# HGRN levels of both directions in one product, and features jobs over side-by-side high and low activations

## The reference

```python
u = h @ w_in                                   # 2048 -> 5 x 2048
q, f_f, f_b, v, g = split(u)
f = lb + (1 - lb) * sigmoid(f_raw);  k = 1 - f # one f and k for each direction
# per head of 128, forward and, on reversed tokens, backward:
#   S_t = diag(f_t) S_{t-1} + k_t v_t^T,  o_t = S_t^T q_t
o = rmsnorm(o_forward + o_backward) * silu(g)
...
up = dwconv3(h @ ffn_w_in);  gate, val = split(up)
x = x + rmsnorm((silu(gate) * val) @ ffn_w_out)
```

## Time and profile before

| | |
|---|---|
| median of 3 runs | 2662.48 us (2662.04 to 2663.64) |
| profiled execution | 2662.26 us, span 2660.5 us |
| PE busy | 2621.0 us (99%) |
| VectorE busy | 1634.4 us (61%) |
| ScalarE busy | 1167.0 us (44%) |
| granted clock of TensorE, mean | 0.996 |
| read from HBM | 461.38 MB, 174 GB/s |

### The profile page before, as it was taken

How to read it: one execution, slowest core, us unless ns; L and a number is a source line. 1 busy time by engine, 2 the same in 40 slices (tenths; PEclk the granted TensorE clock), 3 DMA queues, 4 the chain that set the end, 5 groups by cost and what they waited for, 6 DMA issues and landing times.

```text
span 2660.5 us, 40147 instructions
## 1 busy us (share of the span) xinstructions
PE 2621.0 (99%) x17158; PEld 2391.8 (90%) x17158; DVE 1634.4 (61%) x1811; ACT 1167.0 (44%) x1330; POOL 27.7 (1%) x25
## 2 busy tenths in 40 slices
PE   7999999999999999999999999999899999999997
PEld 6879888998988989989999999988799999999996
DVE  6545656555555555555767667675666666666666
ACT  6544344443443444454333333424445444444443
POOL 0000000000000000000000000000000000000000
PEclk9999999999999999999999999999999999999999
DMA  9534445555555555555444343535455555555553
GB/s 358 170 135 153 159 151 189 182 183 194 185 187 193 183 190 190 182 184 181 143 143 151 127 166 119 181 121 182 143 199 189 183 187 186 184 189 183 186 186 112
DMA packets 127441, 466.09 MB, mean 175 GB/s; under 512 B 14208, under 2 KB 14464, under 8 KB 126368
## 3 DMA queue, kind: packets, MB, share of 16 engines
q1 hardware_dynamic: 127264, 463.54, 50.2%
HBM read 461.38 MB, written 2.10 MB: 174 GB/s over the span
## 4 chain that ended last, share of the span: by engine, by line
PE 67%; issue 32%; ACT 1%; DVE 0%; DMA 0%; POOL 0%; POOLq 0%; DVEq 0%; SPq 0%; ACTq 0%
PE job L676 33%; PE job L679 26%; PE att L861 4%; PE att L808 1%; PE att L708 0%; PE att L696 0%; ACT w_high L928 0%; PE att L872 0%; PE att L886 0%; PE att L889 0%; PE att L849 0%; PE att L776 0%; DMA raw<-in_weights 0%; PE att L726 0%; PE att L749 0%
## 5 line engine op out<-in xcount | busy, mean ns | idle before, releaser
L1176 DVE TENSOR_TENSOR w_low<-raw,w_high 128x1024 fp32r<-128x1024 f32 x856 | 1046.2, 1224 | 914.2 <-ACT w_high L928 912.7
L928 ACT ACTIVATE w_high<-raw 128x1024 fp32r<-128x1024 f32 x856 | 904.6, 1058 | 1258.7 <-PE job L676 638.3
L679 PE MATMUL job<-actA_high,w_high 128*128 128x256 f32 x3328 | 945.5, 284 | 1.0 <-issue 1.0
L679 PE MATMUL job<-actA_high,w_low 128*128 128x256 f32 x3328 | 942.9, 283 | 0.0
L679 PE MATMUL job<-actA_low,w_high 128*128 128x256 f32 x3328 | 942.9, 283 | 0.0
L679 PEld LDWEIGHTS job<-actA_high,w_high 128*128 128x128 f32 x3328 | 639.8, 192 | 2.1 <-issue 1.4
L679 PEld LDWEIGHTS job<-actA_high,w_low 128*128 128x128 f32 x3328 | 639.8, 192 | 0.7
L679 PEld LDWEIGHTS job<-actA_low,w_high 128*128 128x128 f32 x3328 | 639.7, 192 | 0.0
L676 PE MATMUL job<-w_high,actB_high 128*128 128x512 f32 x1184 | 464.4, 392 | 10.7 <-DVE w_low L1176 10.1
L676 PE MATMUL job<-w_low,actB_high 128*128 128x512 f32 x1184 | 462.1, 390 | 0.0
L676 PE MATMUL job<-w_high,actB_low 128*128 128x512 f32 x1184 | 461.8, 390 | 0.0
(11 more groups left out here) (197 smaller groups left out, 1214.2 us busy)
## 6 DMA issues: line engine op xcount, KB each, us to landing
raw<-in_weights SPq DMA_DIRECT2D x856, 512.0 KB, 3.3
M<-in_mem_t SPq DMA_DIRECT2D x4, 512.0 KB, 7.5
slots<-in_mem SPq DMA_DIRECT2D x2, 1024.0 KB, 14.3
M<-in_x_t SPq DMA_DIRECT2D x4, 512.0 KB, 13.2
H<-in_x SPq DMA_DIRECT2D x1, 2048.0 KB, 15.0
out<-H SPq DMA_DIRECT2D x4, 512.0 KB, 2.9
slots<-in_w_small SPq DMA_DIRECT2D x1, 1024.0 KB, 14.4
slots<-in_post_mix_g SPq DMA_DIRECT2D x1, 1024.0 KB, 5.6
```

The lines of the kernel that those rows point to most:

```text
L679: mm = nc.tensor.matmul(J[job.buf][:, x // 2, (x % 2) * T:(x % 2 + 1) * T], wt[:, slot, cc, x * P:(x + 1) * P], a[:, c, :], start=begins a ...
L928: nc.scalar.activation(w_high[:, s % AHEAD, :, :], raw[:, s % RAW_SLOTS, :, :], ACT.Copy)\
L1176: nc.vector.tensor_tensor(w_low[:, s % AHEAD, :, :], raw[:, s % RAW_SLOTS, :, :], w_high[:, s % AHEAD, :, :].bitcast(F32), ALU.subtract).t ...
```

## The change

It has three parts.

1. **Features jobs.** The high and low activations lie side by side for each chunk (`act_both`). Per block of weights, one instruction streams 512 columns (high and low activations) over the high weights, and one streams 256 columns (high activations) over the low weights into the second half of the same PSUM bank. A job has 256 output columns and 4 windows of four chunks; the number of windows stays. The two sums lie in the two halves of a bank and are added when the job is emptied (`join`: ScalarE copies one part to SBUF, VectorE adds the other); a `scale` over both halves follows where there was a product with `R4`.
2. **HGRN levels.** The levels of both directions are one product with 128 columns. The slots of the two directions are swapped so that one access pattern (`crossed`) takes in turn m columns of the one direction's queries and m of the other's; ScalarE copies the keys crossed in the same way into `sq` (`hgrn_keys`). A level stands behind every second window, base+27 to base+39; the stages after it move by two windows.
3. **FFN.** For the value jobs of blocks 1 to 9, `conv_side` moves by two windows, `y_mul` and `y_split` by four.

```diff
-WIN = 2
+        self.width = COLS if kind == "tokens" else T
+        self.per = 1024 // self.width
+        self.windows = len(self.rows) // self.per
...
+def feature_job(p, act, weight, col, needs, to, scaled):
+    for half in (0, 1):
+        j = p.job("features", act, weight, col + half * T, needs=needs)
+        p.put_early(j.end, "join", j.buf, to, half)
+    if scaled:
+        p.put_early(j.end, "scale", to)
+    return j
...
-        for i in range(2 * LEVELS):
-            p.put(base + 27 + i * 12 // 14, "hgrn_level", i // 2, i % 2)
+        for level in range(LEVELS):
+            p.put(base + 25 + 2 * level, "hgrn_keys", level)
+            p.put(base + 27 + 2 * level, "hgrn_level", level)
...
-        p.put(base + 39, "hgrn_across")
+        p.put(base + 41, "hgrn_across")
...
+        later = 2 if which == "value" and 0 < b < FFN_BLOCKS - 1 else 0
         p.put(j.end, "conv_mid", which, b)
-        p.put(j.end + 1, "conv_side", which, b)
+        p.put(j.end + 1 + later, "conv_side", which, b)
...
-            p.put(j.end + 1, "y_mul")
-            p.put(j.end + 2, "y_split", b)
+            p.put(j.end + 1 + 2 * later, "y_mul")
+            p.put(j.end + 2 + 2 * later, "y_split", b)
...
+        def crossed(slot, start, n, m):
+            base = slots[:, slot, start:start + n]
+            return bass.AP(base.tensor, base.offset, [list(base.ap[0]), [2 * m, n // (2 * m)], [1024 + m, 2], [1, m]])
+
+        def block_totals(slot, at, step, n, m):
+            base = slots[:, slot, at:at + 1]
+            return bass.AP(base.tensor, base.offset, [list(base.ap[0]), [2 * m, n // (2 * m)], [step, 2], [0, m]])
...
                         else:
+                            cols = slice(cc * T + x * P, cc * T + (x + 1) * P)
+                            nc.tensor.matmul(J[job.buf][:, x, :], w_high[:, slot, cols],
+                                             act_both[job.act][:, c, :, :].rearrange("p a t -> p (a t)"), start=begins, stop=False,
+                                             skip_group_check=True)
+                            mm = nc.tensor.matmul(J[job.buf][:, x, T:2 * T], w_low[:, slot, cols],
+                                                  act_high[job.act][:, c, :], start=False, stop=ends,
+                                                  skip_group_check=True)
...
-            def hgrn_level(level, direction):
+            def hgrn_level(level):
                 m = 1 << level
+                bank = 2 * (level % 2)
                 wait(pe, n, "diagonal", 0)
-                wait(pe, n, "stepped", -1)
+                wait(pe, n, "stepped", 0)
+                wait(pe, n, "keys_set", 0)
+                wait(pe, n, "picked", -1)
+                wait(pe, n, "o_low", 0)
...
+                        at = (2 * h + t) * P
+                        mm = nc.tensor.matmul(att[:, bank + at // COLS, at % COLS:at % COLS + P],
+                                              hg["sq"][:, at:at + P], crossed(0, h * T + t * P, P, m),
+                                              start=True, stop=True)
...
+                elif name == "join":
+                    buf, to, half_ = a
+                    x = by_feature(JOIN[to][:, half_ * COLS:(half_ + 1) * COLS])
+                    wait(dve, n, "low_copied")
+                    nc.vector.tensor_tensor(x, J[buf][:, :, 0:T], x, ALU.add).then_inc(S["joined"], 1)
+                elif name == "scale":
+                    x = by_feature(JOIN[a[0]])
...
+                    queries, keys = crossed(0, 0, 1024, m), crossed(2, 0, 1024, m)
+                    nc.vector.tensor_tensor(keys, keys, block_totals(7, 2 * m - 1, -1024 - m, 1024, m), ALU.mult)\
+                        .then_inc(S["keys_stepped"], 1)
+                    nc.vector.tensor_tensor(queries, queries, block_totals(6, 2 * m - 1, 1024 - m, 1024, m), ALU.mult)\
                         .then_inc(S["stepped"], 1)
+                    pick = sibling[:, level, :].unsqueeze(1).to_broadcast([P, 8, P])
+                    nc.vector.copy_predicated(heads8(hg["diag"]), pick, att[:, bank:bank + 2, :].rearrange(
+                        "p a (x c) -> p (a x) c", c=P)).then_inc(S["picked"], 1)
                     if level < LEVELS - 1:
-                        double(hg["f"][direction], m)
+                        dve.wait_ge(S["stepped"], n.at("stepped", 1))
+                        t = slots[:, 6:8, :].rearrange("p d (n two m) -> p d n two m", two=2, m=m)
+                        done(nc.vector.tensor_tensor(t[:, :, :, 1, m - 1], t[:, :, :, 0, m - 1], t[:, :, :, 1, m - 1],
+                                                     ALU.mult))
```

More of the change, by code:

```diff
@@ L196, in plan_inputs @@
                       ("gk", GK), ("gv0", GV), ("gv1", GV + COLS), ("gg0", GG), ("gg1", GG + COLS)):
-        j = p.job("features" if name in ("gq", "gk") else "tokens", "A", "w_in", col, needs=("low_made", X_SET))
+        if name in ("gq", "gk"):
+            j = feature_job(p, "A", "w_in", col, None, "gla_" + name[1], True)
+            if name == "gk":
+                p.put_early(j.end, "gla_make")
+            continue
+        j = p.job("tokens", "A", "w_in", col, needs=("low_made", X_SET))
         if name in ("fq", "fk", "mq"):
@@ L275, in plan_hgrn @@
         for direction in (0, 1):
-            j = p.job("features", "A", "hgrn_w_in", (1 + direction) * D + g * COLS, needs=needs)
+            j = feature_job(p, "A", "hgrn_w_in", (1 + direction) * D + g * COLS, needs, f"f{direction}", True)
             if g == 0 and direction == 0:
@@ L340, in up @@
         needs = ("low_made", PREFFN_SET) if b == 0 else None
[L341 to L342 removed]
+        j = feature_job(p, "A", "ffn_w_in", b * COLS + (FFN if which == "value" else 0), needs, "z", True)
+        later = 2 if which == "value" and 0 < b < FFN_BLOCKS - 1 else 0
         p.put(j.end, "conv_mid", which, b)
[L344 removed]
+        p.put(j.end + 1 + later, "conv_side", which, b)
         if which == "gate":
@@ L650, in window @@
                     once(*EMPTIED[job])
-                for cc in range(WIN):
-                    c = job.chunk(WIN * k + cc)
+                for cc in range(job.per):
+                    c = job.chunk(job.per * k + cc)
                     if job.needs:
@@ L659, in window @@
                         elif kind == "y_low":
-                            once(kind, job.rows[WIN * k + cc] // 4 + 1)
+                            once(kind, job.rows[job.per * k + cc] // 4 + 1)
                         elif which == "hgrn":
@@ new lines, in window @@
+                        c = job.rows[job.per * k + cc] % 8
+                    begins = k == 0 and cc == 0
+                    ends = k == job.windows - 1 and cc == job.per - 1
+                    for x in range(TT):
+                        if job.kind == "tokens":
+                            cols = slice(cc * COLS, (cc + 1) * COLS)
+                            ah, al = (a[job.act][:, c, x * P:(x + 1) * P] for a in (act_high, act_low))
+                            to = J[job.buf][:, x, :]
+                            nc.tensor.matmul(to, ah, w_high[:, slot, cols], start=begins, stop=False)
+                            nc.tensor.matmul(to, ah, w_low[:, slot, cols], start=False, stop=False)
+                            mm = nc.tensor.matmul(to, al, w_high[:, slot, cols], start=False, stop=ends)
+                        else:
+                            cols = slice(cc * T + x * P, cc * T + (x + 1) * P)
[5 more added lines that the diff above has]
+                                                  skip_group_check=True)
@@ L1635 @@
                "ffn_w_in": a["ffn_w_in_2"][0], "ffn_w_out": a["ffn_w_out_2"][0]}
-    weights = np.empty((PLAN.windows, P, WIN, COLS), np.float32)
-    for w, (j, k) in enumerate(WINDOW):
-        for cc in range(WIN):
-            r = j.rows[WIN * k + cc]
-            weights[w, :, cc, :] = sources[j.weight][r * P:(r + 1) * P, j.col:j.col + COLS]
+    weights = np.empty((PLAN.windows, P, 1024), np.float32)
+    for w, (job, k) in enumerate(WINDOW):
+        for cc in range(job.per):
+            r = job.rows[job.per * k + cc]
+            weights[w, :, cc * job.width:(cc + 1) * job.width] = (
+                sources[job.weight][r * P:(r + 1) * P, job.col:job.col + job.width])
     def turned(v):
```

205 lines of the change are left out of this document (84 added, 121 removed).

## The result

The changed kernel takes 2603.34 us (median of 4 runs, 2601.59 to 2604.82), the kernel before 2662.66 on the same chips: a ratio of 0.9774 (0.9763 to 0.9786). It is 59.3 us faster; I had said 90. The time lies 11 us above the range of 2565 to 2592. The profiled execution took 2601.59 us at a mean granted clock of 0.996, as before.

A forecast was written before the change was run, and what follows sets the result against it. TensorE's own work was taken as the bound: 2660.5 - 44.3 (features) - 50.8 (HGRN) + 2.0 + 2.5 + 0.8 = 2570.7 us of span, put at 2572.5 us for the time, with an 8-in-10 range of 2565 to 2592.

The forecast's parts named there:

- What bounds the kernel: Whole kernel: TensorE's own work bounds it, busy 2621.0 of 2660.5 us; faster work on other engines can bring little.
- rival D: Joins of the 104 features jobs: buffers not emptied in time, so slower than before, 2718 at 12.5 us an emptying; chance 0.03.
- Features jobs: Features windows: a pair of records costs 0.3467 us instead of 0.360 for three, saving 44.3 us over 3,328 blocks.
- rival C: Features jobs: the pair costs 0.360 us as before, nothing is saved there, and the end is 2617; chance 0.05.
- HGRN levels: HGRN groups: seven merged levels at 1.83 us replace 14 rounds, saving 12.7 us a group, 50.8 for four.
- rival A's small price: HGRN levels: crossed reads are slow at m = 1 alone, +7 us (2579); most of a chance of 0.13.
- VectorE inside the levels: HGRN levels: VectorE needs 7.4 to 6.4 us against 7.3, without delaying levels; the last pick costs 0.5 a group, 2 us.
- the slack of 2.5 us: HGRN levels: VectorE's steps are done at 4.75 us and due at 7.3, so PE does not wait.
- Starts of the features stages: Starts of FFN, MLP and HGRN: PE waits for four activation chunks a window; loss 2.5 us net in FFN, 0.8 elsewhere.
- The 1.40 that the rows product waited: FFN start: the earlier 1.40 us wait for the diagonal absorbs part of the 3.9 us delay, leaving 2.5 net.
- a bound of 11 for the clock: FFN start: if three new 2.4 us waits keep the clock low, each window is 2.8 us longer; bound 0 to +11.
- The FFN move: FFN value jobs: conv sides, y and its split come two to four windows later, at a price of 0.

The follow-up runs named there:

- Experiment 1: Changed kernel with the features jobs set back to three records of 256 columns per block of weights: 2626.04 us, 22.7 us above the changed kernel.
- 5: Changed kernel with the low weights also multiplied with both activations, so every features record has 512 columns: 2927.54 us (one run), 226.7 ns a record.
- 2: Changed kernel with the short record added to the first half of the PSUM bank instead of the second: 2601.27 us, 0.9769 of the kernel before.
- 12: Changed kernel with the record order turned round in every second block (long, short, short, long): 2591.84 us (one run).
- 3: Changed kernel with two long records, then two short ones in each chunk of the features jobs: 2587.28 us, 0.9722 of the kernel before.
- 14: Changed kernel with one more, overwritten 256-column record at the start of each of the 104 features jobs: 2600.49 us (one run).
- 4: Changed kernel with eight long records, then eight short ones in each features window: 2590.97 us, 0.9729 of the kernel before.
- 6: Changed kernel with HGRN level queries read all of one direction, then all of the other, instead of crossed: 2599.84 us, 0.9762 of the kernel before.
- 7: Changed kernel with each HGRN level as two products of 64 columns, one per direction: 2645.89 us, 0.9937 of the kernel before.
- 9: Changed kernel without the move of conv_side, y_mul and y_split in the FFN: 2615.71 us, 0.9823 of the kernel before.
- 8: Changed kernel with the windows of the two halves alternating in the first features jobs of MLP, HGRN and FFN: 2594.88 us, 0.9743 of the kernel before.
- 10: Changed kernel with records grouped by chunk, alternating windows at stage starts, and FFN stages moved in the last block too: 2578.75 us, 0.9681 of the kernel before.
- 13: Changed kernel with chunk-grouped records, alternating start windows, last-block FFN move, and m = 1 read by direction with right pick columns: 2576.47 us, 0.9678 of the kernel before.

## Why the prediction was right or wrong

**What bounds the kernel: right.** No join, no pick and no step became PE's bound; rival D had nothing for it.

**"Features jobs": the step that failed.** The term was 3328 x 0.01333 = 44.3; it measured 3328 x (0.3600 - 0.3533) = 22.2. I had added two prices, 226.7 ns and 120.0, each read in a stream of one length, and argued that "both lengths carry the same surcharge". The result lay between my bounds of 0 and 44.3, yet my range took in rival C only at its zero and gave it 0.05; the middle had no place in it, though I had named it as open ("0 if a switch between lengths costs what is saved"). This one term puts the time at 2594.6, outside the range. Experiment 1 shows the size, 5 that a long record alone costs what I took, 1, 2, 5 and 12 exclude the bank and the columns written, and 3 and 14 show that it hangs on order and on how a stretch begins. The rule that I weighed, 2.5 ns a record and so 8 us ("TensorE: Matmul & The Clock Gate" of the Trainium skill, Back-to-back issue gap), is 14 us too low where the row's 44.3 is 22 too high; the page gives that rule for a lone matmul, and for a stream of weight loads and matmuls it says that both set the spacing. Neither is a price for the mixture. Why the pairs fall into one rhythm or the other stays open.

**"HGRN levels": mechanism right, one price missed.** Merging was said to give 50.8 and gave 4 x (25.5 - 13.6) = 47.6. In that, m = 1 cost 0.88 more than a plain read and m = 2 0.14: (0.88 + 0.14) x 4 = 4.1 us. I had named it at "some 7 us", as rival A's small price, and put it at nothing. It came, at half of the 1.7 that half speed would have cost a level; the others came a little under my 1.83.

**"VectorE inside the levels": size right.** I gave it 2.0; PE's waits there are 0.8. Two prices in it were wrong, though, and the slack of 2.5 us ate them. VectorE's crossed steps at m = 1, then at m = 2 (the timeline):

```profile
1419.93 2.24 DVE L1460 TENSOR_TENSOR slots<-slots 128x1024 f32<-128x1024 f32 x1 [0.29 <-PE att L894]
1422.01 2.28 DVE L1462 TENSOR_TENSOR slots<-slots 128x1024 f32<-128x1024 f32 x1
1424.12 1.32 DVE L1465 COPY_PREDICATED slots<-sibling,att 128x1024 f32<-128x1024 uint8 x1
...
1428.86 1.22 DVE L1460 TENSOR_TENSOR slots<-slots 128x1024 f32<-128x1024 f32 x1
```

I took 1.22 for each; at m = 1 they take 2.24 and 2.28. The pick was said right, at its lower bound.

**"Starts of the features stages": places right, FFN size off.** MLP and HGRN starts: a wait of 0.4 us each, as said, and one of 0.6 more in HGRN, whose releaser the profile doesn't show. At the FFN start I said waits of 2.4, which came as 2.2, but 2.5 us net, which became some 6: the eight windows lost 5.3 and window 591 half a microsecond. Two steps failed. The 1.40 that the rows product waited was to be eaten by the delay, and the wait is still there at 1.4, since the diagonal comes later as well. And the clock: window 592 ran at the lower level (pairs 0.64 us apart) in every kernel, that of before too. The new loss is that the clock fell again in the wait of 2.2 us behind it, and stayed low for most of window 593, some 1.5 us. In experiments 1 to 4, 6, 7, 9 and 12, with the same waits, one or two windows behind the first ran so; in 8, where PE's waits behind the first window are 1.5 and 1.2 us, in 10 and 13, and in the kernel before (1.4 and 1.1), none did. I had a bound of 11 for the clock, and took it at nothing in the 2.5.

**The FFN move: "I give the move 0" was right as a cost and blind to its use.** The move is free, but without it the time is 12.4 us longer (experiment 9). My argument that the joins are hidden looked at the mean share of VectorE, 520 of 715; what counted was the order in its queue behind one window.

## What to carry to other kernels

A price read in a stream of equal instructions isn't the price in a mixture: when a change alternates two lengths, keep every size between "all is saved" and "nothing is saved" in the range, and try the order too (taking two long and then two short records is the same work and gave 16 us here). When producer and consumer come closer at the start of a stage, count the clock, which one wait of 2.2 us dropped again here, and let two halves share each wait. And when an engine with a third of its time free gets more work, read its queue at the one place where another engine waits for it, not its share.

## What was not expected of the hardware

- Pairs of 512 and 256 fp32r columns, each with its weight load, take 346.7 or 353.3 ns a pair, in the same kernel and with the same instructions (8.32 and 8.48 us for three windows in experiment 14). In the slower rhythm the starts lie 233, 117, 241, 120, 236 and 113 ns apart, again and again; in the faster one 230 and 117, again and again; in streams of one length they lie 226.7 and 120.0 apart.
- Operands that change their place at every element cost both VectorE and PE: 2.24 us for 1.22 (VectorE, 1024 elements), 2.66 for 1.78 (PE, 16 records of 128 columns). At blocks of two it is 1.22 on VectorE and 1.92 on PE. Every second element of one slot costs PE nothing (1.82), but a pick that writes every second element costs VectorE 2.47 for 1.32.
- One wait of 2.2 us was enough for the clock to fall from 2.4 to 1.2 GHz for some 3 us of the work behind it (1839.26 to 1842.6); two more waits of 2.2 us in the same stage were not.
